# Half of the first block's conditioning pieces multiplied and summed by GpSimd beside the mixer, with a new order of the first loads and of the steps ahead of the experts

## The reference, cut to what matters

```python
mod = silu(c) @ w_ada + b_ada            # width 6 * 1024, split into shift, scale, gate (mixer), shift, scale, gate (experts)
h = rmsnorm(x, norm1_g) * (1 + scale) + shift
# mixer: attention of 16 heads over the 256 tokens and 256 context tokens,
# and a pooled branch; gated, summed, times w_out
x = x + gate * mixer(h)
# experts: logits = h @ w_router + b_router; top 4; each expert is gate/up, activation, down
x = x + gate2 * experts(rmsnorm(x) * (1 + scale2) + shift2)
```

## Time and profile before

| | us |
|---|---|
| median of 3 runs | 2690.97 |
| lowest and highest run | 2687.77 and 2691.35 |
| the profiled execution, its own time | 2681.76 |
| its span, first to last instruction | 2679.9 |
| TensorE busy in it | 2408.6 |
| VectorE busy | 1243.9 |
| ScalarE busy | 968.1 |
| GpSimd busy | 280.1 |
| moved by DMA | 884.03 MB, 330 GB/s on average |

### The profile page before, as it was taken

How to read it: one execution, slowest core, us unless ns; L and a number is a source line. 1 busy time by engine, 2 the same in 40 slices (tenths; PEclk the granted TensorE clock), 3 DMA queues, 4 the chain that set the end, 5 groups by cost and what they waited for, 6 DMA issues and landing times.

```text
span 2679.9 us, 43667 instructions
## 1 busy us (share of the span) xinstructions
PE 2408.6 (90%) x16394; PEld 1586.1 (59%) x16394; DVE 1243.9 (46%) x3085; ACT 968.1 (36%) x2098; POOL 280.1 (10%) x273
## 2 busy tenths in 40 slices
PE   6989989999999999999988998887778778799997
PEld 5769965555455445555477798442222222388997
DVE  1645532222222222322234756766666665556783
ACT  3343422212212111222132545544444444545762
POOL 0000000000000000000000001444434434100000
PEclk9999989999999999999999999999999999999999
DMA  6666579999999998999937564999999999533552
GB/s 262 255 252 248 205 316 408 422 422 422 422 422 422 422 422 356 422 422 422 421 131 299 223 228 191 422 421 421 421 421 421 421 421 421 243 142 111 189 178 107
DMA packets 121587, 884.03 MB, mean 330 GB/s; under 512 B 13552, under 2 KB 13552, under 8 KB 14192
## 3 DMA queue, kind: packets, MB, share of 16 engines
q1 hardware_dynamic: 83232, 606.11, 56.4%
q0 software_dynamic: 38224, 276.13, 24.8%
HBM read 881.14 MB, written 1.05 MB: 329 GB/s over the span
## 4 chain that ended last, share of the span: by engine, by line
PE 62%; DMA 25%; ACT 5%; DVE 4%; issue 2%; SPq 2%; POOL 0%; ACTq 0%; DVEq 0%; POOLq 0%
PE psum L800 15%; DMA work<-in_uv,work 12%; PE psum L1080 12%; DMA weight_ring<-in_stream 10%; PE psum L1419 7%; PE psum L1112 5%; PE psum L1498 2%; DMA work<-in_stream 2%; PE psum L1033 2%; PE psum L667 2%; SPq L1554 2%; PE psum L1042 2%; PE psum L727 1%; ACT work L2970 1%; ACT work L2577 1%
## 5 line engine op out<-in xcount | busy, mean ns | idle before, releaser
L1419 PE MATMUL psum<-work 128*128 128x512 f32 x1024 | 503.4, 623 | 122.5 <-ACT work L2970 121.8
L1419 PEld LDWEIGHTS psum<-work 128*128 128x128 f32 x1024 | 180.9, 193 | 438.1 <-ACT work L2970 281.4
L2345 DVE CUSTOM_DVE_ANT_0 work<-work 128x1024 f32<-128x1024 f32 x256 | 313.7, 1225 | 220.5 <-DMA work<-in_uv,work 217.1
L2006 DVE TENSOR_TENSOR work<-psum,work 128x256 f32<-128x256 f32 x132 | 56.1, 425 | 690.4 <-PE psum L1053 690.4
L1633 DVE TENSOR_TENSOR ring_parts<-weight_ring,peer_parts 128x1024 fp32r<-128x1024 f32 x218 | 262.5, 1222 | 233.2 <-ACT peer_parts L2633 189.3
L2633 ACT ACTIVATE peer_parts<-weight_ring 128x1024 fp32r<-128x1024 f32 x218 | 224.9, 1053 | 251.4 <-PE psum L800 106.9
L3134 POOL DMA_INDIRECT work<-in_uv,work x256 | 272.7, 1065 | 393.3 <-PE psum L1419 342.6
L1112 PE MATMUL psum<-work 128*64 128x512 f32 x1056 | 244.7, 600 | 25.9 <-ACT work L2801 19.3
L1080 PE MATMUL psum<-weight_ring,work 128*64 128x256 f32 x2112 | 244.9, 382 | 16.6 <-DMA weight_ring<-in_stream 15.7
L1080 PEld LDWEIGHTS psum<-weight_ring,work 128*64 128x64 f32 x2112 | 146.3, 137 | 116.2 <-DMA weight_ring<-in_stream 34.2
L2783 ACT ACTIVATE work<-psum 128x256 f32<-128x256 f32 x132 | 50.6, 383 | 363.3 <-PE psum L1080 363.3
(11 more groups left out here) (326 smaller groups left out, 3374.3 us busy)
## 6 DMA issues: line engine op xcount, KB each, us to landing
weight_ring<-in_stream SPq DMA_DIRECT2D x322, 1024.0 KB, 7.5
work<-in_stream SPq DMA_DIRECT2D x192, 1024.0 KB, 23.6
chunkbuf<-in_stream SPq DMA_DIRECT2D x64, 1024.0 KB, 23.5
work<-in_uv,work POOLq DMA_INDIRECT x256, 22.7
work<-in_rows POOLq DMA_DIRECT2D x1, 1312.0 KB, 16.8
xT<-in_x POOLq DMA_DIRECT2D x1, 1024.0 KB, 9.7
work<-in_ctx POOLq DMA_DIRECT2D x1, 1024.0 KB, 18.7
work<-in_keys POOLq DMA_DIRECT2D x1, 1024.0 KB, 6.3
```

Source lines behind the costliest of these rows:

```text
L1419: mm = pe.matmul(psum[:, 2 * t + h, :], m["diag"][:, g % DIAGS, :], m["rows_of_uv"][row_place[g]][:, D + h * 512:D + (h + 1) * 512], start ...
L2006: ve.tensor_tensor(tb, psum[:, 6, 0:256].rearrange("p (q k) -> p q k", q=4), m["b_gu"][:, slice(b0, b0 + 4) if q is None else bass.ds(b0, ...
L2345: ve.tensor_tensor_reduce(row, row, m["h_nat"][:, t, :], 1.0, 0.0, ALU.mult, ALU.add, m["score"][:, g:g + 1]).then_inc(pick_s, 1)
```

## The change

Of the 48 pieces of `ada1` and `ada2`, 24 (`ada1` 20 to 23, `ada2` 0 to 19) leave the stream for an input of their own, `aside`. GpSimd loads each in two halves of 512 KB, multiplies each of its 8 chunks by the column silu(c), and adds the 8 chunks into one tile of 128 by 512 (as two sums of 4 chunks' halves, 256 columns each). TensorE then needs 2 matmuls per piece instead of 8, against a window with a one in it (`lane`). Three sums are kept. The table `LANES` says after which steps TensorE takes them.

```diff
+BESIDE = {("attn1", k + k // 3): [(1, 8 + k, 9 + k)] for k in range(12)}
+BESIDE["router", 0] = [(2, 20, 23)]
+BESIDE["router", 1] = [(2, 23, 24)]
+ASIDE = [(1, j) for j in range(20, 24)] + [(2, j) for j in range(20)]
+LANES = {("q1", 0): 3, ("q1", 2): 1, ("q1", 3): 1, ("attn1", 0): 1, ("attn1", 2): 1, ("attn1", 4): 1,
+         ("attn1", 6): 1, ("attn1", 8): 1, ("attn1", 10): 1, ("attn1", 13): 1, ("attn1", 15): 1, ("u1", 0): 1,
+         ("u1", 1): 1, ("u1", 2): 1, ("diff", 3): 1, ("pooled", 3): 1, ("ga", 1): 1, ("ga", 2): 1, ("gp", 0): 1,
+         ("gp", 1): 1, ("gp", 3): 1, ("attn_br", 0): 1}
...
+            def lanes(E, *key):
+                for _ in range(LANES.get(key, 0)):
+                    g = len(given)
+                    s, j = ASIDE[g]
+                    given.append(g)
+                    if key == ("u1", 0):
+                        pe.wait_ge(*at("row:mod1b"))
+                    pe.wait_ge(*at(f"aside:{g}"))
+                    for k in range(2):
+                        q = STRIP * (2 * (g % 2) + k)
+                        mm = pe.matmul(psum[q:q + STRIP, 7, 256 * (s == 2):256 * (s == 2) + 256],
+                                       lane[:, STRIP - 1 - j:WINDOW - j], aside_sum[g % SUMS][:, k, :],
+                                       start=(g < 2), stop=True, skip_group_check=True)
+                    mm.then_inc(*E.up(f"ada{s}:{j}"))
...
+            def conditioning_aside(G):
...
+                gp.wait_ge(*at("ada1:7"))
+                load(0, 0)
+                load(0, 1)
+                for g, (s, j) in enumerate(ASIDE):
+                    sums = aside_sum[g % SUMS]
+                    if g >= SUMS:
+                        gp.wait_ge(*at("ada{}:{}".format(*ASIDE[g - SUMS])))
+                    for e in range(2):
+                        gp.wait_ge(aside_in[e], 16 * (g + 1))
+                        for c in range(4):
+                            gp.tensor_scalar(aside_half[e][:, c, :], aside_half[e][:, c, :],
+                                             strips[s][:, 4 * e + c, STRIP - 1:STRIP], None, ALU.mult).then_inc(*G.up())
+                        gp.wait_ge(*G.now())
+                        gp.tensor_tensor(aside_half[e][:, 0:2, :] if e else sums, aside_half[e][:, 0:2, :],
+                                         aside_half[e][:, 2:4, :], ALU.add).then_inc(*G.up())
+                        gp.wait_ge(*G.now())
+                        if e:
+                            gp.tensor_tensor(sums, sums, aside_half[e][:, 0:2, :], ALU.add).then_inc(*G.up(f"aside:{g}"))
+                        if g + 1 < len(ASIDE):
+                            if e:
+                                gp.wait_ge(*G.now())
+                            load(g + 1, e)
```

```diff
-                mean_square("x1", E, m["sq"], DC)
                 bank("ada1", 7)
...
                 conditioning(1, 0, 4, True)
+                mean_square("x1", E, m["sq"], DC)
+                conditioning(1, 4, 8)
+                pe.wait_ge(ident_in, 16)
+                turned_rows("mod1a", 0, E)
+                w_k = piece("k1").rearrange("p (c o) -> p c o", c=DC)
+                pair(w_k, bank("k1x"), hT, DC, "x1").then_inc(*E.up("k1x"))
                 mean_square("ctx", E, m["merged"], DC)
...
+            gp.dma_start(vec[:, :], dram["vec"]).then_inc(vec_in, 16)
             gp.dma_start(xT[:, :, :], dram["x"]).then_inc(x_in, 16)
...
+                gp.wait_ge(*at("ada1:4"))
+                gp.dma_start(m["ctxT"], dram["ctx"]).then_inc(tables_in[1], 16)
                 gp.dma_start(m["rows"], dram["rows1"]).then_inc(tables_in[1], 16)
```

```diff
-            natural(w, ps, hT, E_N, "f1").then_inc(*E.up("router"))
+                for c in range(DC):
+                    q = STRIP * (c % 4)
+                    pe.wait_ge(*at(f"h:f1:{c}"))
+                    mm = pe.matmul(ps[q:q + STRIP, 0:T], w[:, c, :], hT[:, c, :], start=(c < 4), stop=True,
+                                   skip_group_check=True, tile_position=(0, q))
...
+                for h in range(2):
+                    gather(m, h, 6 - h)
+                turned_rows("mod2", 1, E)
...
                 with pe.Fori(0, (TWICE + 1) // 2) as q:
                     for r in range(2):
                         item(q, r, q * 2 + r)
+                biases_of_down(m)
                 with pe.Fori((TWICE + 1) // 2, E_N // 2) as q:
```

270 lines of the change are left out of this document (153 added, 117 removed).

## The result

The changed kernel takes **2787.27 us** (median of 4 runs, 2783.36 to 2787.47), the kernel before 2689.37 beside it (2682.52 to 2691.35): ratio **1.037 [1.035, 1.038]**, slower by 98 us. The forecast was 2673, its range ended at 2698. The profiled execution has a span of 2781.5 us and took 2783.36.

What follows compares the result with a forecast made beforehand. TensorE was taken to bound the mixer, transfers the experts. Terms -12 - 2 - 5 - 5.8 + 7 = -17.8 us gave 2664 for the profiled execution, 2673 on the median of 2690.97; range 2655 to 2698.

Steps and rivals of the forecast that it cites:

- What bounds the kernel: Mixer bound by TensorE, experts by transfers at 422 GB/s; whatever is gained ahead of item 0 arrives at the end in full.
- parts 3 and 4: Start with `vec` loaded first: -5 us. Shorter steps ahead of the experts, second expert's first transfer earlier: net -5.8 us.
- The longer pause at the repeated expert: Down-bias products ahead of item 22, with all 12 places full: transfers pause 3.7 us longer.
- Part 5: GpSimd's own pace: 9.0 us a piece, bounds 6.5 and 15.7; TensorE then hardly waits for sums.
- The prediction's own sign: Forecast is wrong if TensorE's idle time names GpSimd for more than 10 us.
- The breakpoint of 9.5 us: GpSimd's slowest pace per piece that still suffices: (270 - 71) / 21.
- The price of 21 us: Time lost for each 1 us of GpSimd's pace per piece above 9.5 us.
- Rival C: GpSimd too slow, TensorE waits for its sums; at 11 us a piece +7, 2698 us; chance 15%.
- upper bound of 15.7: GpSimd's slowest pace per piece in us, taken with `vec`'s landing time of 11.5 us.
- Parts 1 and 2: TensorE drops 24 conditioning pieces at 1.0 us, adds 24 sums at 0.5: -12. Fewer ring waits in `u1`: -2.
- Part 6: VectorE held up beside GpSimd in the attention, five instructions per pair at about 0.3 us: +7 us, ends 0 and +63.
- The cover of part 4: Block 2's first 4 pieces, requested later, have some 15 us until its keys start; without that cover 5 us.

Runs made afterwards that it cites:

- e6: Changed kernel with nothing on GpSimd and the start of the kernel before, only the steps ahead of the experts new: 2681.42 us, ratio 0.998.
- e1: Changed kernel with all 24 pieces back on TensorE and nothing on GpSimd, new start and expert steps kept: 2675.23 us, ratio 0.996.
- e14: Changed kernel with 8 matmuls by zero weights on TensorE ahead of each wait for a sum, from the fourth on: 2793.3 us, ratio 1.040.
- e17: Changed kernel without GpSimd's multiplications (sums leave out silu), timed and traced a second time: 2669.38 us, ratio 0.994.
- e9: Changed kernel with 16 pieces on GpSimd instead of 24, two-input multiplies, down-bias products after item 16: 2688.29 us, ratio 1.001.
- e15: Changed kernel with six pieces on GpSimd, only after the attention, two-input multiplies, down-bias products after item 16: 2672.8 us, ratio 0.996.
- e16: Changed kernel with nothing on GpSimd and the down-bias products after item 16 instead of 21: 2671.54 us, ratio 0.995.
- e10: Changed kernel with 12 pieces on GpSimd, starting late in the attention, two-input multiplies, down-bias products after item 16: 2673.41 us, ratio 0.994.
- e4: Changed kernel with GpSimd multiplying two chunks per two-input instruction against a broadcast column, 4 instructions a piece instead of 8: 2711.99 us, ratio 1.009.
- e5: Kernel before, with unused GpSimd arithmetic of six pieces beside the attention and single instructions of several forms: 2687.16 us, ratio 1.001.
- e3: Changed kernel without GpSimd's multiplications; adds, loads and semaphores stay, so sums leave out silu: 2669.44 us, ratio 0.994.

## Why the prediction was wrong

**What bounds the kernel, and parts 3 and 4: right.** The mixer is bound by TensorE in the kernel before (though the row for the 20 large pieces covers 86 of their 121 us). `q1` was forecast at 65 and came at 65.5. Its terms were off one by one: the keys of x start at 32.3 and not at 28, and the mean square of the context takes 3.5 us and not 1.5; the first did not matter, as TensorE was to stand there in any case, and context and `rows`, waited for together, had landed at 39.2 (about 40). Item 0 came 27.5 us behind the mean square (28.5), the second expert's first transfer 30.6 (32). By themselves (e6, e1) the two parts gave 5.7 and 6.2 us, against 5.8 and 5. The longer pause at the repeated expert is 13.6 - 10.6 = 3.0 us (3.7).

**Part 5, GpSimd's pace: the step that failed.** The sum took 9.0 us a piece, with a multiply of 256 elements at 0.425 us, VectorE's price of a copy, and an add at 1.0; what bound it was the round of a half, landing included. Measured are 0.917 for the multiply (median; 1.05 the mean beside VectorE) and 1.26 for the add (means 1.34 to 1.6): undisturbed a piece takes 13.2 us (from the multiplies at 74.63 to those at 87.79), in the mean 14.6. The eight multiplies alone are 8.3 us where the sum had 3.4. The 1.4 us from 13.2 to 14.6, some 34 us over 24 pieces, are a second price that the sum had at nothing: GpSimd's instructions last longer beside VectorE's, as the last add of the first piece, 3.20 us from 54.25, while VectorE works from 53.35 to 62.15; the prediction counted only VectorE as held up. The round trip of the load, which the text feared, takes 4.2 us and was hidden behind the other half from the second load on: GpSimd's own arithmetic is the bound, a limit that the forecast put at 3.4 + 3.0 + 1.1 = 7.5 us and so below the round. The prediction's own sign came true: TensorE's idle time names GpSimd for 89.8 us, and not under 10.

The breakpoint of 9.5 us was about right, though no run had that pace. Three kernels (14.6, 11.9 and, in e14, 14.8 us a piece) have the mean square at 43 + 24 x pace + 66.5 us, within 0.5 us (the pace being the time to the last sum by 24, what the three share is the 66.5); e17, which never waits for a sum, has it at 344.6, which this line reaches at 9.8. The price of 21 us for each microsecond above it was too low: at 14.6 us a piece the three places for sums never hold GpSimd up, so all 24 pieces count. The forecast's model gives 21 x (14.6 - 9.5) = 107 us lost against 25 gained, 2773; from e17 the line gives 2669.4 + 24 x (14.6 - 9.8) = 2785, and the run gave 2787.

**Rival C named the mechanism but was priced at 11 us a piece, near its threshold,** while the same text had an upper bound of 15.7 for the pace. At that bound C gives 21 x 6.2 - 25 = +105, 2796 us. A bound that stands in the sum has to stand in the range too. And the reasons for and against C, which made it 15%, speak of transfers and of VectorE alone; what GpSimd's arithmetic costs, the one price without a row, was not weighed there.

**Parts 1 and 2: right, once the pace is made harmless.** A sum costs TensorE 0.56 us at full clock (280.60 to 281.16 in e17; 0.5). By the steps of the forecast the mean square comes at 355.4 - 12 - 2 - 5 + 7 = 343.4; in e17, the change without the multiplications, it comes at 344.6, and the time is 2669.4. Against e1 (351.2) the pieces aside bring 6.6 us there, the forecast's net -7; in the medians 5.8. `u1` took 27.8 us (27).

**Part 6: the number fits e17, and that is partly luck.** The attention took 65.7 us and not the 60 to 64 that were forecast; by TensorE's work alone it would be 60 (3.75 us a pair), so some 5.7 of the 7 us were lost. But GpSimd only adds in e17, and is busy for 38.55 of 71 us; the forecast had it busy for 7.5 of each 9. The loss was taken at 0.3 us for each of five steps; in e17 the scaling lost 0.16 and the step with `vec` 0.38. In e9, with the multiplies in (GpSimd busy for 55.83 of 82 us), the scaling lost 0.48, and the scores took 76.7 us where TensorE's work is 67.6 - 24 + 16 + 3.5 = 63: 13.6 us lost. So the forecast of 2673 is near the time of a kernel whose GpSimd adds and does not multiply; that a GpSimd of 9.0 us a piece, multiplying, would have given it is not shown, and e9 speaks against it. Of the miss itself nearly all is the pace: the mean square was forecast at 343.4 and came at 459.4. That is 116 of the 119 us by which the profiled execution missed its 2664.

**The cover of part 4 ("cost at nothing") held:** no transfer is among TensorE's waits of 0.6 us or more from 1439 to 1738 us in the changed kernel. But the stretch behind the second expert's first transfer is 8.5 us longer in the changed kernel (2781.5 - 490.0 against 2679.9 - 396.95), of which 0.7 to the mean square of block 2. In e1, e6, e15 and e16 what lies behind the mean square of block 2 is 1 to 5 us longer than before. The work there is the same; in one such stretch of 140 us the granted clock is 0.95 for 0.99. Part of it may be the executions compared: the one before lay 9 us under its median, that of the changed kernel 4. What sets it was not tried and stays open.

## What to carry to other kernels

Before work is moved to another engine, its pace there decides, and another engine's row doesn't give it: where no row shows it, take the whole span up to the worst bound into the range, or time one instruction of the exact form first. An engine that hands over items at a fixed pace, slower than they are wanted, sets the end by the number of items times the pace, and filling the gaps so that the clock came back did not change that (e14). Once the pace is mended, the next limit is the engine that the helper disturbs: here a VectorE step that starts with a GpSimd add lasted as long as the whole add, and with GpSimd multiplying too the pieces aside gained nothing (e9, e10, e15). So price each step that the helper can strike at up to the helper's whole instruction.

## What the runs showed of the hardware

- GpSimd in fp32: `tensor_scalar` of 128x256 0.92 us and of 128x1024 2.84 by a column, with VectorE idle, 2.77 by an immediate; `tensor_tensor` of 128x512 1.26 (the shortest in the changed kernel) to 1.33, of 128x1024 2.35; with a broadcast column as second operand, 128x512, 1.05 (median in e4). For 1024 elements a multiply of one input took longer than an add of two. The Trainium skill (GPSIMD Engine Reference, Engine selection) gives one-input operations there as roughly line rate; the rows differ, and they decide: VectorE scales 512 elements in 483 ns, where 2 x 924 ns are needed here.
- A GpSimd issue of a load waits 0.30 us for the add before it and takes 0.6 us, 1.8 us a piece.
- VectorE beside GpSimd (changed kernel, e9): scaling of 512 elements 0.76 and 0.96 us for 0.48, the step with `vec` 0.42 and 0.49 for 0.16; the reduction from PSUM 1.22 in all. As long as TensorE had more work this cost nothing (e5).
- TensorE's granted clock: 0.50 for 4 us of full work after a stretch of 8 us with 0.22 us of work (the changed kernel), and after an idle time of 2.80 us (e3); 0.94 to 0.99 when the same gaps were filled with products by zero. Two executions of one kernel (e3, e17) differ by 14 us, with 0.91 and 0.79 against 1.00 and 0.93 in attention and `u1`.
